# Shared expert of the eight even prompt tiles as four blocks of 256 tokens behind the last routed expert, with the last norm between them

## The chip, the cores and the metric

The kernel runs on one core of a Trainium2 chip. The metric is the device time of one execution in microseconds; the median of three executions is compared.

## The reference, cut to what matters

One layer of a decoder over 2048 prompt tokens and 64 sample tokens of width 1024: a mixer (sliding-window attention and short convolution), a norm, a mixture of experts with one shared expert, a second norm. The change concerns the last two:

```
xt = layer_norm(ALPHA * x + mixer(x))
shared = (silu(xt @ ws_gate) * (xt @ ws_up)) @ ws_down          # 1024 -> 256 -> 1024, every token
routed = sum over the 6 chosen of 64 experts of gate * ((silu(xt @ w_gate[e]) * (xt @ w_up[e])) @ w_down[e])
y = layer_norm(ALPHA * xt + routed + shared)
```

All is float32. A product is made of float32r parts: each operand is split in a high part (rounded, on ScalarE) and a low part (the difference, on VectorE), and high x high, high x low and low x high are summed.

## The kernel before, in words

Tokens lie in 17 tiles of 128 (16 of the prompt, one with the 64 sample tokens). There are four stages, one behind the other, each with its own program per engine and signals between the engines: the mixer, the dense stage, the routed experts, the norm. Every engine works its program in order; the order within a stage is written out by hand.

The dense stage (`stage_dense`) makes step i for tile i. TensorE's order in a step: first half of the output projection of tile i+1 (`project`, 24 products of 512 columns), transposes of the hidden values of tile i-1 (`hidden_T`), transposes of h of tile i (`transpose_h`), second half of the projection, the rank sums of tile i-1 (`rank`), the shared expert's down product of tile i-1 (`down`, 12 products), the router product (`router`), the shared expert's gate and up of tile i (`gate_up`, 24 products of 512 columns), the router's logits (`logits`). VectorE's: split of the hidden values (`hidden`, L1209), split of h (`split_h`, L1198), `ranks` (L1251), `residual` and mean of tile i+1, split of the next cat tile, `accumulate` of tile i-1 (acc = ALPHA * h + shared), `normalise` of tile i+1, `place` (slots of tile i-1 in the routing table), `activate` (sigmoid x gate x up, L1203), `pick` (the choice of experts, L1220 to L1249). ScalarE rounds, scales, and makes sigmoids and square roots. SP loads x and cat of the next tiles and stores acc to `acc_d`; GpSimd stores h to `h_d` and scatters the entries to the table. Steps 1 to 14 are a hardware loop of seven rounds with an odd and an even step; step 0 and the last two tiles are written out.

The expert stage (`stage_experts`) runs 64 experts in pairs, each on up to 256 gathered tokens: rows of `h_d` are gathered by GpSimd, transposed, split; gate and up in two halves f (L1927, L1929: 16 times 512 and 256 columns for 256 tokens), then down (L1905 to L1907) for two token tiles and two column halves, whose sums ScalarE scales (`output`, L1751) and GpSimd adds to `acc_d` by indirect DMA. The chain behind a half is `copy_lo` (L1711, ScalarE), `sums` (L1818), `sigmoid` (ScalarE), `activate`, `hidden` on ScalarE (rounding) and on VectorE (rest). Weights come from memory by SP, 1 MB in each transfer, are rounded by ScalarE (L1733) and split by VectorE (L1842). Behind the loop over pairs (`pairs`) stand the last two experts' ends: L1978 to L1993 for TensorE.

The norm stage (`stage_norm`) starts when all routed sums are in memory and every engine has left the expert stage. SP loads tiles of `acc_d`, ScalarE makes sum and squares of a tile (`statistics`, L2057), VectorE subtracts the mean and multiplies by g (`centre`, L2087), then multiplies by the reciprocal deviation and adds b (`finish`, L2096), SP stores to y. TensorE and GpSimd have no part in it.

## Time and profile before

| | us |
|---|---|
| median of three executions | 2157.96 (2151.61 to 2160.45) |
| profiled execution, own time | 2153.67 |
| its span, first to last instruction | 2151.8 |
| TensorE busy in it | 2041.9 (95%) |
| VectorE, ScalarE, GpSimd busy | 1406.2, 1224.3, 624.8 |

The profile comes from one execution. A timeline row gives the start, the length, the engine (PE TensorE, PEld its weight loads, DVE VectorE, ACT ScalarE, POOL GpSimd, SP the DMA queue of SyncE), the line of the kernel, what is written and read; in brackets how long the engine had been idle and what ended it. Matmuls overlap: their starts tell the pace, not their lengths. The mean granted TensorE clock is 0.978 of full speed.

### The profile page before, as it was taken

What the parts mean: (1) busy time and instruction counts of PE and PEld (TensorE: products, weight loads), DVE (VectorE), ACT (ScalarE), POOL (GpSimd) and SP (SyncE); (2) the same over time, 40 slices, a digit from 0 to 9 for tenths busy, and PEclk for the clock granted to TensorE, in tenths of its full rate; (3) what the DMA queues carried; (4) which work ended last, traced back from release to release, by engine and by line L of the source; (5) the groups of instructions that cost most, each with busy time, mean ns of one, the idle gap of its engine ahead of it and who ended that gap; (6) DMA issues with size and microseconds to landing.
All of it is one profiled execution on the core that took longest, in us unless ns stands there. A gap on an engine that the chain in (4) does not pass through costs nothing. (4 is left out here: it accounts for less than half of the span.)

```text
span 2151.8 us, 36827 instructions
## 1 busy us (share of the span) xinstructions
PE 2041.9 (95%) x11526; PEld 1717.9 (80%) x11526; DVE 1406.2 (65%) x2774; ACT 1224.3 (57%) x2167; POOL 624.8 (29%) x659
## 2 busy tenths in 40 slices
PE   8999999999999999988999999999999999999950
PEld 6777787787778888876888888889988888888840
DVE  6444444444667777777777777777777777776628
ACT  6344344343543333334777777776777777766628
POOL 2111111111013232243444444354333333333210
PEclk9999999999999999999999999999999999999975
DMA  5101101010453232345999999999999999999857
GB/s 223 56 31 37 44 30 37 30 40 32 171 199 118 78 117 78 116 159 176 273 285 306 301 307 292 302 299 293 282 283 294 304 294 284 287 291 280 246 121 300
DMA packets 113978, 413.82 MB, mean 192 GB/s; under 512 B 35872, under 2 KB 40480, under 8 KB 86208
## 3 DMA queue, kind: packets, MB, share of 16 engines
q1 hardware_dynamic: 76032, 290.02, 37.1%
q0 software_dynamic: 37872, 122.90, 24.5%
q8 instruction: 36, 0.59, 0.1%
q14 instruction: 38, 0.31, 0.0%
HBM read 316.91 MB, written 98.12 MB: 193 GB/s over the span
## 5 line engine op out<-in xcount | busy, mean ns | idle before, releaser
L1927 PE MATMUL ex_psU<-ex_xs,ex_guh 128*128 128x384 f32 (+5 forms) x2016 | 621.9, 372 | 0.1
L1929 PE MATMUL ex_psU<-ex_xs,ex_gul 128*128 128x192 f32 (+5 forms) x2016 | 522.6, 259 | 0.0
L1927 PEld LDWEIGHTS ex_psU<-ex_xs,ex_guh 128*128 128x128 f32 x2016 | 378.0, 187 | 49.0 <-issue 17.7
L1929 PEld LDWEIGHTS ex_psU<-ex_xs,ex_gul 128*128 128x128 f32 x2016 | 384.1, 191 | 1.5
L1688 POOL DMA_INDIRECT ex_xg<-h_d,entries x128 | 156.9, 1226 | 486.7 <-issue 238.5
L1671 POOL DMA_INDIRECT acc_d<-ex_y,ex_rows x128 | 215.9, 1687 | 200.8 <-ACT ex_y L1751 172.3
L1751 ACT ACTIVATE ex_y<-ex_psY,ex_use 128x512 f32<-128x512 f32 x254 | 169.8, 682 | 50.9 <-PE ex_psY L1958 26.1
L1818 DVE TENSOR_TENSOR ex_gu<-ex_psU,ex_lo 128x384 f32<-128x384 f32 (+5 forms) x128 | 77.3, 604 | 170.6 <-ACT ex_lo L1711 170.5
L1905 PE MATMUL ex_psY<-ex_dnh,ex_hdh 128*128 128x512 f32 (+3 forms) x412 | 171.7, 417 | 8.5 <-DVE ex_dnl L1842 4.3
L1847 DVE TENSOR_TENSOR ex_xs<-ex_psX,ex_xs 128x512 fp32r<-128x512 f32 (+5 forms) x125 | 130.7, 1046 | 58.8 <-ACT ex_xs L1740 57.8
L720 PE MATMUL mi_psG<-mi_gh,mi_xh 128*128 128x512 f32 x408 | 167.7, 411 | 0.0
L1711 ACT ACTIVATE ex_lo<-ex_psU 128x384 f32<-128x384 f32 (+5 forms) x128 | 66.9, 523 | 173.6 <-PE ex_psU L1929 173.0
L1907 PE MATMUL ex_psY<-ex_dnh,ex_hdl 128*128 128x512 f32 (+3 forms) x412 | 163.7, 397 | 0.0
L1906 PE MATMUL ex_psY<-ex_dnl,ex_hdh 128*128 128x512 f32 (+3 forms) x412 | 162.9, 395 | 0.0
L1842 DVE TENSOR_TENSOR ex_gul<-mi_g_raw,ex_guh 128x1024 fp32r<-128x1024 f32 x128 | 156.0, 1221 | 10.1 <-ACT ex_guh L1733 10.1
L1842 DVE TENSOR_TENSOR ex_gul<-mi_g_place,ex_guh 128x1024 fp32r<-128x1024 f32 x128 | 156.0, 1221 | 7.8 <-ACT ex_guh L1733 7.4
L720 PE MATMUL mi_psG<-mi_gl,mi_xh 128*128 128x512 f32 x408 | 159.7, 392 | 0.0
L720 PE MATMUL mi_psG<-mi_gh,mi_xl 128*128 128x512 f32 x408 | 159.7, 391 | 0.0
L1733 ACT ACTIVATE ex_guh<-mi_g_raw 128x1024 fp32r<-128x1024 f32 x128 | 134.0, 1049 | 11.1 <-PEq L900 11.1
L1733 ACT ACTIVATE ex_guh<-mi_g_place 128x1024 fp32r<-128x1024 f32 x128 | 134.0, 1049 | 0.0
L1913 PE MATMUL ex_psX<-ex_ident,ex_xg 128*128 128x128 f32 x1008 | 130.9, 273 | 2.0 <-DMA ex_xg<-h_d,entries 1.8
L1740 ACT ACTIVATE ex_xs<-ex_psX 128x512 fp32r<-128x512 f32 (+5 forms) x125 | 110.3, 883 | 31.4 <-PE ex_psX L1913 30.2
(411 smaller groups left out, 4241.3 us busy)
## 6 DMA issues: line engine op xcount, KB each, us to landing
mi_g_raw<-w_experts SPq DMA_DIRECT2D x96, 1024.0 KB, 8.0
mi_g_place<-w_experts SPq DMA_DIRECT2D x96, 1024.0 KB, 7.9
mi_xr<-xT SPq DMA_DIRECT2D x17, 512.0 KB, 3.6
acc_d<-de_acc SPq DMA_DIRECT2D x17, 512.0 KB, 3.0
h_d<-de_h POOLq DMA_DIRECT2D x17, 512.0 KB
de_cr<-cat SPq DMA_DIRECT2D x16, 512.0 KB, 6.0
de_xr<-x_rows SPq DMA_DIRECT2D x16, 512.0 KB, 5.3
mi_g_raw<-w_conv SPq DMA_DIRECT2D x6, 1024.0 KB, 16.0
```

The source lines that it names most:

```text
L720: last = nc.tensor.matmul(psG[:, (k + j) % 2, :], a[:, k, kc, :], b[:, j, kc, :], start=(kc == 0 and n == 0), stop=(kc == KC - 1 and n == 2))
L1671: nc.gpsimd.indirect_dma_start(out=io["acc_d"], out_offset=bass.IndirectOffsetOnAxis(ap=rows[0:r, 2 * b + t:2 * b + t + 1].bitcast(U32), a ...
L1688: nc.gpsimd.indirect_dma_start(out=xg[0:r, k, :], out_offset=None, in_=io["h_d"], in_offset=bass.IndirectOffsetOnAxis(ap=ent[0:r, k, 0:1]. ...
L1733: A(hi, src, ACT.Copy).then_inc(s_round if q < 4 else s_dround, 1)
L1751: A(y[0:r, k, half * 512:(half + 1) * 512], sums(u)[at], ACT.Copy, scale=use[at, k, 1:2].bitcast(F32)).then_inc(s_y, 1)
L1842: V.tensor_tensor(lo, src, hi.bitcast(F32), ALU.subtract).then_inc(done, 1)
L1905: nc.tensor.matmul(out, lh, rh, start=start, stop=False)
L1906: nc.tensor.matmul(out, lh, rl, start=False, stop=False)
L1907: return nc.tensor.matmul(out, ll, rh, start=False, stop=stop)
L1913: last = nc.tensor.transpose(rows_T(p, t)[:, kc * P:(kc + 1) * P], xg[:, 2 * b + t, kc * P:(kc + 1) * P], ident[:])
L1927: nc.tensor.matmul(psU[:, f, half, 0:2 * n].rearrange("p (s n) -> p s n", s=2), guh[:, b, kc, c0:c0 + P], rows_split(e)[:, kc, :, 0:n], st ...
L1929: last = nc.tensor.matmul(psU[:, f, half, 0:n], gul[:, b, kc, c0:c0 + P], rows_split(e)[:, kc, 0, 0:n], start=False, stop=(kc == KC - 1))
```

## The change

In the dense stage the even prompt tiles (0, 2, ... 14, `DEFERRED`) no longer run gate and up, hidden and down of the shared expert. `keep_h` on ScalarE writes ALPHA * h for them to acc, and SP stores their split h (high and low, 1 MB for each tile) to a new memory tensor `hT_d`. Odd tiles and the sample tile keep the shared expert; m counts them.

Behind the last routed expert the shared weights are loaded, rounded and split like a 65th expert's, and four blocks of two deferred tiles run (`gate_up_block`, `down_block`). TensorE's order is now gate_up of the last expert, down of the last two, and then (n, f being block and half) G00 G01 G10 D0 G11 G20 D1 G21 G30 G31 D2 D3. The norm stage is gone as a stage; its work stands between the chains of the blocks:

- ScalarE: chains 00, 01, 10; `statistics` 1, 3, 5; `deviations` 0; chain 11; `squares` 0, 2; deviations 1; chain 20; statistics 7, 9; squares 4, 6; deviations 2; chain 21; statistics 11; chain 30; statistics 13; chain 31; statistics 15, 16; deviations 3; squares 8, 10; deviations 4; squares 12, 14; deviations 5.
- VectorE: chains 00, 01, 10; `add` 0, 2; `reciprocals` 0; `scale` 1, 3, 5; chain 11; reciprocals 1; scale 0, 2; chain 20; add 4, 6; `centre` 4, 6; reciprocals 2; scale 7, 9; chain 21; `finish` 4, 6; chain 30; centre 13; chain 31; add 8, 10; centre 15, 16; reciprocals 3; scale 11; finish 13; add 12; finish 16, 15; centre 8, 10; reciprocals 4; finish 8; add 14; finish 10; centre 12, 14; reciprocals 5; finish 12, 14.
- GpSimd multiplies by g and adds b for the eight tiles that VectorE scaled (`ON_POOL`).

```diff
+BLOCKS = PT_TILES // 4
+DEFERRED = range(0, PT_TILES, 2)
+STATS = (1, 3, 5, 0, 2, 7, 9, 4, 6, 11, 13, 15, 16, 8, 10, 12, 14)
+BATCHES = (3, 5, 9, 13, 15, 17)
+ON_POOL = (1, 3, 5, 0, 2, 7, 9, 11)
+ON_DVE = (4, 6, 13, 16, 15, 8, 10, 12, 14)
+STORES = (1, 3, 5, 0, 2, 4, 6, 7, 9, 11, 13, 16, 15, 8, 10, 12, 14)
+LOADS = ((0, 2), (1, 3), (5, 7), (4, 6), (9, 11, 8, 10), (13, 15, 12, 14, 16))
...
+            def store_hT(i, n):
+                sp.wait_ge(S["hT_lo"], i + 1)
+                sp.dma_start(io["hT_d"][bass.ds(n, 1)].rearrange("o p n -> (o p) n"),
+                             hT[:].rearrange("p k s t -> p (k s t)").bitcast(F32)).then_inc(S["hT_stored"], 16)
...
+            def step(i, k, first, m):
                 if not first:
                     load_x(i + 1)
                 load_cat(i + 2)
+                if k == 0:
+                    store_hT(i, 0 if first else m + 1)
                 if not first:
                     store_acc(i - 1, acc)
...
+            def step(i, k, first, m):
                 if first:
                     scale_attention(1)
+                elif k == 0:
+                    hidden(m, psR[:, 128:384])
+                if k == 0:
+                    round_h(i, psT[:], "gu", 0 if first else m + 1)
                 else:
...
+            def keep_h(i):
+                act.wait_ge(S["acc_stored"], 16 * i)
+                A(acc[:], h[:, 0, :], ACT.Copy, scale=ALPHA).then_inc(S["acc"], 1)
...
+                if k == 1:
+                    keep_h(i - 1)
                 copy_router(i)
                 deviation(i + 1)
                 score(i)
-                sigmoid(i, psU[:, 0:FF])
+                if k == 1:
+                    sigmoid(m, psU[:, 0:FF])
...
                 project(i + 1, 1 - k, 0)
                 if first:
                     project(1, 1, 1)
                     pe.wait_ge(S["zero"], 2)
+                elif k == 0:
+                    hidden_T(i - 1, m, psR[:, 128:384])
                 else:
-                    hidden_T(i - 1, psR[:, 128:384])
                     after(pe, S["acc"], i - 1)
                 transpose_h(i, k, psT)
                 if not first:
                     project(i + 1, 1 - k, 1)
-                    pe.wait_ge(S["hid_lo"], i)
+                    if k == 0:
+                        pe.wait_ge(S["hid_lo"], m + 1)
                     rank(i - 1)
                     pe.wait_ge(S["hT_lo"], i + 1)
-                    down(i - 1, psT)
+                    if k == 0:
+                        down(m, psT)
                 else:
                     pe.wait_ge(S["w_lo"], n_w - 1)
                 router(i)
-                gate_up(psU[:], range(KC)).then_inc(S["gu"], 1)
+                if k == 1:
+                    after(pe, S["hid"], m)
+                    gate_up(psU[:], range(KC)).then_inc(S["gu"], 1)
                 logits(i)
                 if first:
                     pe.wait_ge(S["w_lo"], n_w)
...
+            for kind in range(2):
+                hold(sp, s_split, 4 * e - 6 + 2 * kind, s_sp_passed)
+                load_shared(kind)
             load_down(e - 1, 1)
+            hold(sp, s_dsplit, 2 * e - 2, s_sp_passed)
+            load_shared(2)
+            hold(sp, s_split, 4 * e - 2, s_sp_passed)
+            sp.dma_start(ln_g[:], io["ln2_g"].partition_broadcast(P)).then_inc(s_const, 16)
+            sp.dma_start(ln_b[:], io["ln2_b"].partition_broadcast(P)).then_inc(s_const, 16)
+            hold(sp, s_xT, 2 * e, s_sp_passed)
+            load_block(0)
+            hold(sp, s_gu, 2 * e, s_sp_passed)
+            load_block(1)
             hold(sp, s_add, 32 * e, s_sp_passed)
+            load_tiles(0)
+            load_tiles(1)
+            hold(sp, s_gu, 2 * e + 2, s_sp_passed)
+            load_block(2)
+            for n in range(2, 5):
+                load_tiles(n)
+            hold(sp, s_gu, 2 * e + 4, s_sp_passed)
+            load_block(3)
+            hold(sp, s_split, 4 * e + 2, s_sp_passed)
+            load_tiles(5)
+            for i in STORES:
...
+                sp.dma_start(io["y"][i * P:i * P + rows_at(i)], t_of(i)).then_inc(s_stored, 16)
+            sp.wait_ge(s_stored, 16 * TILES)
...
+            pool.wait_ge(s_const, 48)
+            for n, i in enumerate(ON_POOL):
+                pool.wait_ge(s_scaled, n + 1)
+                nc.gpsimd.tensor_tensor(t_of(i), t_of(i), ln_g[:], ALU.mult)
+                pool.drain()
+                nc.gpsimd.tensor_tensor(t_of(i), t_of(i), ln_b[:], ALU.add).then_inc(s_pout, 1)
...
+            def statistics(i):
+                r = rows_at(i)
+                act.drain()
+                act.wait_ge(*tiles_loaded(count, i))
+                A(scratch[0:r], t_of(i), ACT.Copy, accum_out=of(total, i))
+                act.drain()
+                A(of(minus, i), of(total, i), ACT.Copy, scale=-1.0 / D)
+                act.drain()
+                squares(i)
+            def squares(i):
+                if i in DEFERRED:
+                    act.drain()
+                    act.wait_ge(s_added, DEFERRED.index(i) + 1)
+                A(scratch[0:rows_at(i)], t_of(i), ACT.Square, bias=of(minus, i), accum_out=of(square, i)).then_inc(s_square, 1)
+            def deviations(n):
+                at = slice(BATCHES[n - 1] if n else 0, BATCHES[n])
+                act.drain()
+                A(std[:, at], square[:, at], ACT.Sqrt, bias=eps, scale=1.0 / D).then_inc(s_std, 1)
...
+            def add(n, c):
+                i = DEFERRED[2 * n + c]
+                dve.wait_ge(s_dn, 4 * (e + n) + 2 * c + 2)
+                dve.wait_ge(*tiles_loaded(count, i))
+                V.scalar_tensor_tensor(t_of(i), psX[:] if c else psY[:].rearrange("p h n -> p (h n)"), 1.0, t_of(i),
+                                       ALU.mult, ALU.add, accum_out=of(total, i))
+                dve.drain()
+                V.tensor_scalar(of(minus, i), of(total, i), -1.0 / D, None, ALU.mult).then_inc(s_added, 1)
+            def centre(i):
+                dve.wait_ge(s_square, STATS.index(i) + 1)
+                V.scalar_tensor_tensor(t_of(i), t_of(i), of(minus, i), ln_g[0:rows_at(i)], ALU.add, ALU.mult)
+            def reciprocals(n):
+                at = slice(BATCHES[n - 1] if n else 0, BATCHES[n])
+                dve.wait_ge(s_std, n + 1)
+                V.reciprocal(rstd[:, at], std[:, at])
+                dve.drain()
+            def scale(i):
+                V.tensor_scalar(t_of(i), t_of(i), of(minus, i), of(rstd, i), ALU.add, ALU.mult).then_inc(s_scaled, 1)
+            def finish(i):
+                V.scalar_tensor_tensor(t_of(i), t_of(i), of(rstd, i), ln_b[0:rows_at(i)], ALU.mult, ALU.add).then_inc(s_out, 1)
...
+            def gate_up_block(n, f):
+                x = x_block(n)
+                if f == 0:
+                    pe.wait_ge(s_block[n % 2], 16 * e + 32 * (n // 2) + 32)
+                pe.wait_ge(s_sum, 2 * (e + n) + f - 1)
+                for half in range(2):
+                    c0 = half * FF + f * P
+                    for kc in range(KC):
+                        if n == 0 and f == 0 and half == 0 and kc % 2 == 0:
+                            pe.wait_ge(s_split, 4 * e + kc // 2 + 1)
+                        nc.tensor.matmul(psU[:, f, half, :].rearrange("p (s c t) -> p s c t", s=2, c=2), guh[:, 0, kc, c0:c0 + P],
+                                         x[:, :, kc].rearrange("p c s t -> p s c t"), start=(kc == 0), stop=False)
+                        last = nc.tensor.matmul(psU[:, f, half, 0:BLK].rearrange("p (c t) -> p c t", c=2), gul[:, 0, kc, c0:c0 + P],
+                                                x[:, :, kc, 0, :], start=False, stop=(kc == KC - 1))
+                last.then_inc(s_gu, 1)
+            def down_block(n):
+                pe.wait_ge(s_hl, 2 * (e + n) + 2)
+                if n == 0:
+                    pe.wait_ge(s_dsplit, 2 * e + 2)
+                    pe.wait_ge(s_y, 4 * e)
+                for c in range(2):
+                    if n:
+                        pe.wait_ge(s_added, 2 * n - 1 + c)
+                    for half in range(2):
+                        out = psX[:, half * 512:(half + 1) * 512] if c else psY[:, half, :]
+                        for f in range(FC):
+                            last = three(out, hdh[:, n % 2, f, c * P:(c + 1) * P], hdl[:, n % 2, f, c * P:(c + 1) * P],
+                                         dnh[:, 0, f, half * 512:(half + 1) * 512], dnl[:, 0, f, half * 512:(half + 1) * 512],
+                                         f == 0, f == FC - 1)
+                        last.then_inc(s_dn, 1)
+            gate_up(e - 1, 1, 1, BLK)
             for t in range(2):
                 down(e - 2, 0, t, BLK)
-            gate_up(e - 1, 1, 1, BLK)
...
+            for t in range(2):
+                down(e - 1, 1, t, BLK)
+            gate_up_block(0, 0)
+            gate_up_block(0, 1)
+            gate_up_block(1, 0)
+            down_block(0)
+            gate_up_block(1, 1)
+            gate_up_block(2, 0)
+            down_block(1)
+            gate_up_block(2, 1)
+            gate_up_block(3, 0)
+            gate_up_block(3, 1)
+            down_block(2)
+            down_block(3)
```

## Rows read from the trace of the kernel before

**Rows 1.** Windows: length, busy PE, PEld, DVE, ACT, POOL, granted clock, DMA share, GB/s
```profile
2054.40:2064.40 10.00, 5.86 (x14) 4.61 (x15) 1.97 (x4) 2.35 (x5) 0.00 (x0) 0.66 0.39 89
...
2085.00:2098.00 13.00, 0.00 (x0) 0.00 (x0) 0.00 (x2) 0.58 (x2) 3.04 (x2) 0.63 0.72 169
...
2098.00:2151.80 53.80, 0.00 (x0) 0.00 (x0) 46.91 (x58) 43.69 (x94) 0.00 (x0) 0.50 0.78 300
```

**Rows 2.** TensorE's timeline, one dense step (start, length, engine, line, out<-in, shape, count)
```profile
899.85 0.20 PE L1425 MATMUL de_psR<-de_mkb,de_trib 128*128 128x64 bf16 x1
...
899.92 0.48 PE L1398 MATMUL de_psT<-de_dnh,de_hdh 128*128 128x512 f32 x1
...
902.80 1.11 PE L1450 MATMUL de_psR<-de_hT,de_rw 128*128 128x256 f32 x8
...
903.75 0.39 PE L1398 MATMUL de_psU<-de_guh,de_hT 128*128 128x512 f32 x1
...
909.21 0.55 PE L1457 MATMUL de_psR<-de_eye,de_lt 128*128 128x64 f32 x4
...
915.15 0.38 PE L1433 MATMUL de_psR<-de_ident,de_hid 128*128 128x128 f32 x2
...
915.37 1.04 PE L1419 MATMUL de_psT<-de_ident,de_h 128*128 128x128 f32 x8
...
916.16 0.48 PE L1398 MATMUL de_psC<-mi_gh,mi_xh 128*128 128x512 f32 x1
...
921.73 0.20 PE L1425 MATMUL de_psR<-de_mkb,de_trib 128*128 128x64 bf16 x1
```

**Rows 3.** VectorE's timeline in that step; in brackets what it waited for
```profile
900.19 0.23 DVE L1254 TENSOR_TENSOR de_dd<-de_psR,de_base 128x64 f32<-128x64 f32 x1 [3.35 <-PE de_psR L1426]
...
911.33 0.42 DVE L1205 TENSOR_TENSOR de_hid<-de_psU,de_sg 128x256 f32<-128x256 f32 x1
...
912.16 0.22 DVE L1222 TENSOR_TENSOR de_sel<-de_sc,de_rbias 128x64 f32<-128x64 f32 x1
...
916.55 0.42 DVE L1211 TENSOR_TENSOR de_hdl<-de_psR,de_hdh 128x256 fp32r<-128x256 f32 x1
```

**Rows 4.** ScalarE's timeline in that step
```profile
903.95 0.38 ACT L1105 ACTIVATE de_lt<-de_psR 128x256 f32<-128x256 f32 x1 [6.42 <-PE de_psR L1450]
...
907.12 1.28 ACT L1110 ACT_TABLE_LOAD   x1
```

**Rows 5.** TensorE's timeline at the dense stage's two ends
```profile
625.02 0.50 PE L1398 MATMUL de_psA<-mi_gh,mi_xh 128*128 128x512 f32 x1 [0.33 <-DVE mi_xl L1164]
...
939.09 0.47 PE L1398 MATMUL de_psC<-mi_gh,mi_xh 128*128 128x512 f32 x1
...
947.44 1.11 PE L1450 MATMUL de_psR<-de_hT,de_rw 128*128 128x256 f32 x8
```

**Rows 6.** TensorE's timeline behind the routed loop
```profile
2058.54 0.79 PE L1905 MATMUL ex_psY<-ex_dnh,ex_hdh 128*128 128x512 f32 x1 [4.15 <-issue]
...
2064.55 0.39 PE L1907 MATMUL ex_psY<-ex_dnh,ex_hdl 128*128 128x512 f32 x1
```

**Rows 7.** Timelines of ScalarE and VectorE, first half of the last routed expert
```profile
2054.43 0.60 ACT L1711 ACTIVATE ex_lo<-ex_psU 128x512 f32<-128x512 f32 x1 [3.92 <-PE ex_psU L1929]
...
2055.15 0.69 DVE L1818 TENSOR_TENSOR ex_gu<-ex_psU,ex_lo 128x512 f32<-128x512 f32 x1 [3.15 <-ACT ex_lo L1711]
```

**Rows 8.** Timelines of ScalarE and VectorE in the norm
```profile
2129.98 1.04 ACT L2060 ACTIVATE ln_scratch<-ln_t 128x1024 f32<-128x1024 f32 x1
...
2132.76 0.29 ACT L2066 ACTIVATE ln_std<-ln_square,ln_eps 128x1 f32<-128x1 f32 x1
...
2147.17 1.28 DVE L2097 SCALAR_TENSOR_TENSOR ln_t<-ln_t,ln_rstd,ex_ln_b 64x1024 f32<-64x1024 f32 x1
```

**Rows 9.** GpSimd's group of its widest operation; VectorE's timeline, one cast
```profile
L348 POOL TENSOR_TENSOR mi_pr<-mi_pr,mi_rd 128x1024 f32<-128x1024 f32 x16 | 30.3, 1893 | 135.0 <-DVE mi_rd L582 135.0
...
612.61 0.22 DVE L1302 CAST de_trib<-de_trif 128x128 bf16<-128x128 f32 x1
```

435 lines of the change are left out of this document (236 added, 199 removed).

## The prediction

> **What bounds the kernel now.** Start with the windows of the last stretch [rows 1]: from 2085 on TensorE runs nothing. For 13 us the last routed sums are added to memory and a stage boundary is crossed, then the norm takes 53.8 us with VectorE busy 46.91 and ScalarE 43.69. Then read TensorE's timeline over one step of the dense stage [rows 2]: rank, down, router, gate and up, logits, output projection and transposes follow each other without a hole, 21.88 us from rank to rank (899.85 to 921.73). VectorE in the same step waits 3.35 us [rows 3]. So the dense stage is bound by TensorE, the tail by VectorE and ScalarE, and the change moves work from the one to the other. What it is worth is the dense time saved minus the growth of the tail.
>
> **Dense stage: what a step loses.** An even tile no longer runs gate and up, 903.75 to 909.21 = 5.46 us, nor, in the odd step behind it or the even step behind that, its transposes of hidden (915.15 to 915.37 = 0.22) and its down product (899.92 to 902.80 = 2.88 with the rank's tail) [rows 2]. Eight tiles at some 8.5 us would be 68 us; what is late next takes part of it back.
>
> Odd step, whose tile keeps gate and up but has no down and no hidden transpose of the tile before. The down product used to hide the round trip from rank to router: VectorE reads the ranks 0.34 us behind the rank and needs 0.22 [rows 3], so the router can start 0.66 behind it. From there, [rows 2]: router 0.95, gate and up 5.46, logits and first half of the projection 5.94 (909.21 to 915.15), the hidden transpose of this odd tile 0.22, transposes 0.79, second half 5.57. Sum 19.59 from rank to rank.
>
> Even step: down of the odd tile 2.95, router 0.95, then the logits at once, which need ScalarE's copy: 903.95 + 0.38 stands 1.53 behind the router's start [rows 4], with some 0.1 for the signal 1.63, so 0.68 is waited. Then 5.94 + 0.79 + 5.57. Sum 16.88.
>
> Is VectorE still ahead? From a rank to the end of pick it takes 16.70 us now (899.85 to 916.55), 0.83 of it activate (911.33 to 912.16) [rows 3]. Even step: 15.87, then split_h 1.2 (1024 columns, as in [rows 8]), done at 17.1, while TensorE's next rank starts at 16.88 and VectorE is wanted at 17.22. It is covered by 0.1 us only. The odd step has 1.8 us to spare. If nothing covers, each tenth late costs a tenth in six steps. ScalarE's new keep_h (a copy of 1024 columns, 1.04 as its like in [rows 8]) lies in its 6 us wait for the router. The new store of 1 MB sits in SP's queue ahead of the store of acc and the loads of the next x and cat; it starts before the rank and those are issued some 7 us behind it, so it is through. GpSimd's six scatters per step are behind the table as before.
>
> Ranks of steps 1 to 14 are 13 periods apart: now 13 x 21.88 = 284.4, then 7 x 19.59 + 6 x 16.88 = 238.4. That is **46.0 us**. Step 0 gives nothing for its 5.46: the next projection waits for VectorE's split of cat at 625.02 anyway [rows 5]; the missing hidden transpose of step 1 gives 0.2. Behind step 14 the second half of the last projection starts 17.36 us behind the rank (921.73 to 939.09); then it waits for the mask of tile 14, at 15.3: 2.1 us. Behind it down(14) goes from in front of the router (947.44) [rows 5] and ScalarE's deviation comes about 1 us sooner. Dense stage together **49.3 us**; from both sides 43 (VectorE a full microsecond late in each even step) to 53 (the waits of 0.66 and 0.68 not seen).
>
> **Tail, step by step**, on the clock of the profile before, without the dense gain.
> - TensorE stops 4.15 us at the end of the routed loop [rows 6] and then runs at half clock (granted 0.66 on average in the window from 2054.4 [rows 1]) until some 5.9 us behind the restart; 512 columns take 0.23 us at full clock (5.46 / 24 [rows 2]) and twice that or a little less at half. The hole stays, since the loop stays. gate_up of the last expert, now first, takes 8.3 at that clock, the four down units of each of the two last experts 11.0 and 0.7 of waits for ScalarE's copies: the blocks start at 2078.5. The second hole (to 2077) is gone.
> - A block's gate and up is twice 16 x 768 columns = 2 x 5.5, its down 24 x 512 = 5.5 (columns as in [rows 2]). Alone, TensorE would be done at 2078.5 + 66 = 2144.8.
> - A chain of one block half is copy 0.60, sums 0.69 [rows 7], then sigmoid, two products, rounding, split of 256 columns at 0.42 each [rows 3]: about 3.6 us over two engines. The statistics of a tile cost ScalarE 2.78 (2129.98 to 2132.76), the squares alone 1.3 [rows 8], each change between sigmoid and square root a table of 1.28 [rows 4]. VectorE: add 1.3 and 0.15, centre and finish 1.2 each [rows 8]. scale, with one tensor input, was not seen at this size; the cast of 128 columns in 0.22 costs what 64 would at the rate of the 256-column rows, so I take 0.69, not 1.2 [rows 3, 9].
> - ScalarE is through chain (1,0) at 2098.4. Three statistics 8.4, table and root 1.6: 2108.4. VectorE waits for that root, scales three tiles, and only then does chain (1,1): down of block 1 starts at 2113.9 instead of 2111.7.
> - Roots for tiles 0 and 2 at 2117.6, chain (2,0) done 2122.3, adds to 2125.3; ScalarE's two statistics and two squares to 2130.0, root 2131.6; centre twice, scale twice, sums (2,1) at 2134.0. TensorE's gate_up (3,1) waits for it, 3.5 us, and loses 2.3 at half clock: 2141.9.
> - Chain (2,1), finish twice, chain (3,0), centre(13) behind its statistics (2146.0), chain (3,1) to 2149.1, adds to 2152.1. Down of block 3 starts at 2150.6 and ends at 2158.4.
> - From there VectorE's queue has one hole of 0.9 us: 13 centres and finishes, two adds, a scale and three reciprocals, 21.3 us: 2173.4. The last store lands 3.4 behind, as now (finish from 2147.17 to 2148.45, span 2151.8 [rows 1, 8]): **2177.0**, a tail 25.2 us longer.
> - GpSimd's two operations per tile (1.89 each [rows 9]), sixteen in all, run beside VectorE. No row has a two-input VectorE operation under such a one. Bounds: 0, or they exclude each other; then most chain links from (1,1) to (3,0) wait 1.2 to 1.9 and the walk ends at 2185.4, 8.4 later. Nothing in the rows leans to either end, so I take the middle, 4.2.
>
> The Trainium skill, "SBUF — State Buffer", section "Who interferes with whom", says that a VectorE instruction with two SBUF inputs and a GpSimd instruction that reads SBUF block each other for the whole instruction. No run here shows it yet. By it the sum takes the upper end, 8.4, instead of 4.2.
>
> **Sum.** 2151.8 - 49.3 + 25.2 + 4.2 = 2131.9 of span. The profiled execution took 2153.67 around its span of 2151.8, so 2133.8. It lies 4.3 below the median of the three runs (2157.96); on the median's scale 2138.
>
> **Rivals.**
> - Full exclusion of VectorE and GpSimd in the tail: 4.2 more, **2142**. For it: VectorE and GpSimd both read SBUF tiles all through the tail. Against: nothing in the rows.
> - The dense stage turns to VectorE: 0.1 us of cover in the even steps. At 43 us saved, **2144**. For it: the thin cover and the drains of the loop's end; against: VectorE's step repeats to a hundredth.
> - The tail stays close to TensorE: waits for tables and statistics overlap better than in my walk, tail 15 longer instead of 29: **2124**. Against: both queues are in order, and ScalarE and VectorE are already at 44 and 47 of 54 us with the norm alone [rows 1].
> - Slower than before: transfers set the tail. From 2063 to the end 8.4 MB of blocks, 8.7 MB of tiles and 8.7 MB of stores go through the 16 engines. The norm moved 300 GB/s on average, the stretch of scattered adds just before 169 [rows 1]. Below 186 GB/s the bytes alone end the tail behind 2201, where the dense gain is used up; at 169 they end at 2215, which gives **2172**. Against: only the first loads meet scattered adds, and the norm's rate holds with loads and stores together.
>
> **Numbers.** Forecast 0.50, full exclusion 0.20, dense turned to VectorE 0.12, short tail 0.08, transfers 0.10. Bounds together: dense 53 and tail 16 gives 2121, dense 43 and tail 38.6 (upper end of GpSimd, scale at 1.2) gives 2154. Range 2118 to 2156. A measurement of this kernel can tell about 0.5%, 10.8 us, from no change. Faster than 2147.2: nearly all of the first and of the short tail, most of the two between: 0.79. Within: 0.12. Slower: 0.09, the transfers.
>
> **What would show it.** In the dense stage, rank to rank alternating 19.6 and 16.9 instead of 21.88, the router waiting for VectorE in odd steps and the logits for ScalarE in even ones; VectorE's wait before the ranks close to nothing in even steps. In the tail, TensorE starting blocks some 24 us behind the loop's end and idle three times (before down 1, gate_up (3,1), down 3) by 2 to 5 us with its clock halved behind the longer ones; VectorE the engine without holes at the end; GpSimd's operations near 1.9 us if nothing excludes, longer, or VectorE's two-input ones longer, if it does. Wrong would be: no alternation in the dense stage (the gain fell to VectorE), waits of ScalarE on loads in the tail (transfers), or TensorE ending last with the stores.

## The result, and the profile after

The changed kernel takes **2172.56 us** (median of 12 runs, 2165.5 to 2178.11), the kernel before 2157.66 (12 runs beside them, 2150.01 to 2166.84): ratio 1.0069, 95% interval 1.0052 to 1.0086. It is 0.7% slower, some 15 us. The forecast was 2138, its range 2118 to 2156. In what follows a ratio to the kernel before is turned into microseconds by 2157.7; a difference between two changed kernels goes over two such ratios and is known to some 5 us.

The profiled execution has a span of 2172.4 us where the sum said 2131.9, so 40.5 us are to be found. They can be split at marks that both traces have (the first routed product is the first product of the routed experts):

| us | before | after | change | predicted |
|---|---|---|---|---|
| start of the dense stage | 591.47 | 594.24 | +2.8 | 0 |
| from there to the first rank | 45.74 | 48.06 | +2.3 | -0.2 |
| 13 periods, rank to rank | 284.5 | 252.0 | -32.5 | -46.0 |
| to the last rank | 46.11 | 47.76 | +1.7 | -3.1 |
| to the first routed product | 27.0 | 28.3 | +1.3 | 0 |
| from there to the first block | - | 1080.3 | | 1083.7 |
| first block to the end | - | 121.7 | | 102.7 |

The predicted 1083.7 and 102.7 are the forecast's block start at 2078.5 and tail end at 2181.2, on the clock of before, whose first routed product is at 994.8. The first line isn't the change: the other profiled executions, whose kernels are alike up to there, start the dense stage at 591.1 to 591.8 or at 593.7 to 594.7. The first routed product comes 24.4 us earlier than before; without the 2.8 of the start the dense stage gave 27.2 of the 49.3 us (in one execution). The last line costs 19 us more than foreseen.

TensorE's timeline over an even step and the odd one behind it (columns: start, duration, engine and line, operation, out<-in, count, idle before it and what ended it), to be read against [rows 2, 4]:

```profile
778.18 0.20 PE L1455 MATMUL de_psR<-de_mkb,de_trib 128*128 128x64 bf16 x1
...
781.14 1.11 PE L1479 MATMUL de_psR<-de_hT,de_rw 128*128 128x256 f32 x8
782.72 0.66 PE L1486 MATMUL de_psR<-de_eye,de_lt 128*128 128x64 f32 x4 [0.47 <-ACT de_lt L1122]
784.69 0.50 PE L1428 MATMUL de_psA<-mi_gh,mi_xh 128*128 128x512 f32 x1 [1.31 <-DVE mi_xl L1191]
...
796.62 0.20 PE L1455 MATMUL de_psR<-de_mkb,de_trib 128*128 128x64 bf16 x1
...
797.33 1.19 PE L1479 MATMUL de_psR<-de_hT,de_rw 128*128 128x256 f32 x8 [0.48 <-DVE de_dd L1285]
...
816.35 0.20 PE L1455 MATMUL de_psR<-de_mkb,de_trib 128*128 128x64 bf16 x1
```

The alternation is there: odd 19.73 (predicted 19.59), even 18.44 (predicted 16.88). The logits' wait of 0.47 was in the sum; the 1.31 in front of the projection was not. VectorE's queue in the same even step shows where it comes from:

```profile
778.52 0.23 DVE L1285 TENSOR_TENSOR de_dd<-de_psR,de_base 128x64 f32<-128x64 f32 x1 [2.38 <-PE de_psR L1456]
779.18 1.28 DVE L1198 SCALAR_TENSOR_TENSOR de_t<-de_psC,de_rc,de_t 128x1024 f32<-128x1024 f32 x1 [0.33 <-issue]
780.59 1.23 DVE L1202 SCALAR_TENSOR_TENSOR de_t<-de_xr,de_t 128x1024 f32<-128x1024 f32 x1
...
782.22 1.28 DVE L1207 SCALAR_TENSOR_TENSOR de_centred<-de_t,de_minus,mi_g_raw 128x1024 f32<-128x1024 f32 x1
783.42 1.22 DVE L1191 TENSOR_TENSOR mi_xl<-de_cr,mi_xh 128x1024 fp32r<-128x1024 f32 x1
```

The split of cat (mi_xl) for the tile after next stands behind ranks, residual and centre, and ends 6.5 us behind the rank. TensorE is there after 5.2. Two of the six even steps took 20.05 and 20.08: in them the clock fell behind that wait. The windows of the stretch behind the wait, of such a step and of the one above (columns as in [rows 1]; PEclk is the first figure behind the busy times):

```profile
744.90:751.00 6.10, 6.10 (x20) 4.87 (x21) 5.45 (x30) 2.23 (x4) 1.01 (x2) 0.72 0.67 214
784.60:790.00 5.40, 5.31 (x23) 4.43 (x24) 4.83 (x23) 2.33 (x4) 0.58 (x1) 1.00 0.62 199
```

Step 0 and the end of the stage, TensorE's timeline, against [rows 5]:

```profile
627.72 0.80 PE L1428 MATMUL de_psA<-mi_gh,mi_xh 128*128 128x512 f32 x1 [4.11 <-DVE mi_xl L1191]
...
909.23 0.20 PE L1455 MATMUL de_psR<-de_mkb,de_trib 128*128 128x64 bf16 x1 [1.81 <-DVE de_mkb L1274]
...
923.20 1.66 PE L1449 MATMUL de_psA<-de_ident,de_h 128*128 128x128 f32 x8 [3.33 <-DVE de_h L1219]
...
931.42 2.04 PE L1479 MATMUL de_psR<-de_hT,de_rw 128*128 128x256 f32 x8 [3.40 <-DVE de_dd L1285]
```

Before, the same projection of step 0 waited 0.33 [rows 5]. At the end the forecast's first gain is there: the second half of the last projection starts 15.0 us behind its rank (909.30) where it was 17.36, and 15.3 was said. Then it is lost again. The last two waits have their like in the kernel before, 0.99 and this one:

```profile
960.03 1.19 PE L1450 MATMUL de_psR<-de_hT,de_rw 128*128 128x256 f32 x8 [3.04 <-DVE de_dd L1254]
```

What is new is the clock behind them. Windows from that router to the last rank, before (one) and after (two, columns as above):

```profile
960.03:967.84 7.81, 7.31 (x39) 6.00 (x40) 4.86 (x38) 1.38 (x4) 3.65 (x4) 1.00 0.54 221
```

```profile
931.42:937.10 5.68, 5.68 (x18) 4.81 (x18) 2.10 (x17) 0.38 (x1) 1.96 (x2) 0.50 0.69 280
937.10:942.06 4.96, 4.26 (x22) 3.31 (x21) 2.93 (x20) 0.99 (x3) 3.88 (x4) 0.99 0.03 3
```

In the tail TensorE's three holes are at the three named places (down of block 1, gate_up (3,1), down of block 3), but 8 to 10 us long where 2 to 5 were said:

```profile
2093.31 0.79 PE L2175 MATMUL ex_psY<-ex_dnh,ex_hdh 128*128 128x512 f32 x1 [8.30 <-DVE ex_hdl L2014]
...
2120.99 0.80 PE L2260 MATMUL ex_psU<-ex_x_odd,ex_guh 128*128 128x512 f32 x1 [8.63 <-DVE ex_gu L1997]
...
2143.63 0.76 PE L2175 MATMUL ex_psY<-ex_dnh,ex_hdh 128*128 128x512 f32 x1 [9.50 <-DVE ex_stats L2092]
```

VectorE's queue around the first hole and a little later, then GpSimd's over that later stretch:

```profile
2085.80 0.17 DVE L2101 RECIPROCAL ex_stats<-ex_stats 128x3 f32<-128x3 f32 x1 [11.07 <-ACT ex_stats L1947]
...
2102.72 1.46 DVE L2003 TENSOR_TENSOR ex_gu<-ex_gu,ex_lo 128x256 f32<-128x256 f32 x1 [0.48 <-ACT ex_lo L1830]
2104.25 2.47 DVE L2008 TENSOR_TENSOR ex_gu<-ex_gu 128x256 f32<-128x256 f32 x1
2107.29 1.98 DVE L2014 TENSOR_TENSOR ex_hdl<-ex_gu,ex_hdh 128x256 fp32r<-128x256 f32 x1 [0.56 <-ACT ex_hdh L1837]
2109.19 1.21 DVE L2089 SCALAR_TENSOR_TENSOR ex_t<-ex_psY,ex_t 128x1024 f32<-128x1024 f32 x1
```

```profile
2101.04 2.85 POOL L1813 TENSOR_TENSOR ex_t<-ex_t,ex_ln_g 128x1024 f32<-128x1024 f32 x1
...
2104.04 2.40 POOL L1815 TENSOR_TENSOR ex_t<-ex_t,ex_ln_b 128x1024 f32<-128x1024 f32 x1
2106.40 2.58 POOL L1813 TENSOR_TENSOR ex_t<-ex_t,ex_ln_g 128x1024 f32<-128x1024 f32 x1
2109.12 2.42 POOL L1815 TENSOR_TENSOR ex_t<-ex_t,ex_ln_b 128x1024 f32<-128x1024 f32 x1
```

An operation on 256 columns that takes 0.42 alone takes 1.46 to 2.47 here: each of the three ends 0.28 to 0.29 us behind the end of a GpSimd instruction. The add at 2109.19, which reads one operand from PSUM, runs in its 1.21 right through GpSimd's. And in the first line VectorE stands 11.07 us in front of the first reciprocal, with a finished product of TensorE waiting behind it in the queue.

### The profile page after: what moved, and what is told of

The parts are those of the page before. It is cut to its first block, busy times and chain, and to the rows that moved or that the text cites. A ratio compares the mean times of both kernels' runs of the same rounds, so it can differ in the third digit from the quotient of the medians.

```text
span 2172.4 us, 37064 instructions
## 1 busy us (share of the span) xinstructions
PE 2063.9 (95%) x11574; PEld 1735.0 (80%) x11574; DVE 1420.0 (65%) x2780; ACT 1243.9 (57%) x2169; POOL 679.4 (31%) x675
## 4 chain that ended last, share of the span: by engine, by line
PE 49%; DVE 2%; DMA 2%; ACT 1%; issue 1%; DVEq 1%; SPq 0%; ACTq 0%; POOL 0%; POOLq 0%
PE ex_psU L2197 20%; PE ex_psU L2199 9%; PE ex_psX L2183 5%; PE ex_psY L2177 4%; PE ex_psY L2175 4%; PE ex_psY L2176 4%; PE ex_psY L2228 2%; DMA acc_d<-ex_y,ex_rows 1%; DMA ex_t<-acc_d 1%; ACT ex_scratch L1942 0%; DVE ex_t L2105 0%; DVE ex_t L2108 0%; DVE ex_t L2096 0%; ACT ex_scratch L1932 0%; DVE ex_gu L2008 0%
## 5 line engine op out<-in xcount | busy, mean ns | idle before, releaser
L1795 POOL DMA_INDIRECT ex_xg<-h_d,entries x128 | 161.8, 1264 | 492.2 <-issue 267.0
L1778 POOL DMA_INDIRECT acc_d<-ex_y,ex_rows x128 | 221.2, 1728 | 179.0 <-ACT ex_y L1865 139.9
L2175 PE MATMUL ex_psY<-ex_dnh,ex_hdh 128*128 128x512 f32 (+3 forms) x432 | 179.9, 416 | 18.3 <-DVE ex_stats L2092 9.5
L1865 ACT ACTIVATE ex_y<-ex_psY,ex_use 128x512 f32<-128x512 f32 (+5 forms) x256 | 171.1, 682 | 40.5 <-PE ex_psY L2228 26.1
L1997 DVE TENSOR_TENSOR ex_gu<-ex_psU,ex_lo 128x512 f32<-128x512 f32 (+5 forms) x136 | 82.7, 608 | 170.4 <-ACT ex_lo L1825 170.3
L1825 ACT ACTIVATE ex_lo<-ex_psU 128x512 f32<-128x512 f32 (+5 forms) x136 | 71.6, 527 | 180.5 <-PE ex_psU L2199 172.0
L2177 PE MATMUL ex_psY<-ex_dnh,ex_hdl 128*128 128x512 f32 (+3 forms) x432 | 171.6, 397 | 0.0
L2176 PE MATMUL ex_psY<-ex_dnl,ex_hdh 128*128 128x512 f32 (+3 forms) x432 | 170.8, 395 | 0.0
L2021 DVE TENSOR_TENSOR ex_gul<-mi_g_raw,ex_guh 128x1024 fp32r<-128x1024 f32 x132 | 160.6, 1219 | 13.7 <-ACT ex_guh L1847 13.7
```

What stands on the lines that cost most here:

```text
L1778: nc.gpsimd.indirect_dma_start(out=io["acc_d"], out_offset=bass.IndirectOffsetOnAxis(ap=rows[0:r, 2 * b + t:2 * b + t + 1].bitcast(U32), a ...
L1795: nc.gpsimd.indirect_dma_start(out=xg[0:r, k, :], out_offset=None, in_=io["h_d"], in_offset=bass.IndirectOffsetOnAxis(ap=ent[0:r, k, 0:1]. ...
L1865: A(y[0:r, k, half * 512:(half + 1) * 512], sums(u)[at], ACT.Copy, scale=use[at, k, 1:2].bitcast(F32)).then_inc(s_y, 1)
L2021: V.tensor_tensor(lo, src, hi.bitcast(F32), ALU.subtract).then_inc(done, 1)
L2175: nc.tensor.matmul(out, lh, rh, start=start, stop=False)
L2176: nc.tensor.matmul(out, lh, rl, start=False, stop=False)
```

## Experiments

Twelve kernels, each timed against the kernel before on the same chip. "First block to end" is read from the one profiled execution of a kernel; where the work behind the first block is the changed kernel's (runs 2 and 3) it is 120.8 and 121.3 for 121.7.

**1. The dense half alone** (dense_alone). The expert and norm stages are those of the kernel before; the dense stage is the changed one.

```
-        stage_experts(nc, io, ov, front["raw"], first_entries, s_ent, s_weights, s_sp_passed, s_passed)
+        first = stage_experts(... of the kernel before ...)
+        stage_norm(nc, io, first, s_norm)
```

> The dense stage of the changed kernel (with the store of hT) in front of the expert and norm stages of the kernel before; the shared expert of the eight even tiles is left out. It prices the first half of the change by itself. Theory: in an even step the next projection waits for VectorE's split of cat, which stands behind ranks, residual and centre in its queue; the loop gives back 32.5 us and the first step and the end lose 5 to 8 of it, so 2132 us (24 to 27 under before), and the tail then has cost the changed kernel 39 to 42 us. Rival, my prediction's account: the dense stage gives 49 us and the changed kernel lost all of it behind, 2109 us.

Measured 2118.53 us, ratio 0.9841 (0.9803 to 0.9879): 34 us under the kernel before, 26 to 42 with the interval. More than the 24 to 27 expected, less than the forecast's 49. The expectation rested on one execution, whose 24.4 held 2.8 us of a late start and more of a lowered clock: in this run's profile the dense stage up to the first routed product gives 32.1 us where the changed kernel's gave 27.2, and 2.5 of the difference lie behind the last router, where the clock stayed at 1.00 (8.11 us to the last rank for 10.64). The tail of the changed kernel has then cost (1.0069 - 0.9841) x 2157.7 = 49 us, where the forecast had 29.

**2. The split early in every step** (cat_first).

```
                 else:
+                    split_cat(i + 2, k)
                     ranks(i - 1)
                 residual(i + 1)
-                split_cat(i + 2, k)
```

> The changed kernel with VectorE's split of cat for tile i+2 moved ahead of ranks (into 2.4 us in which VectorE sits idle). Theory (place of the split): TensorE's 1.31 us wait before the projection goes in 7 steps, and with it the two steps in which the clock then fell (1.6 us each): even period 18.44 to 17.1, 9 to 13 us faster than the changed kernel, 2160 to 2163 us. Rival: another wait (the router's copy, the mask, the h of the next tile) takes its place, under 4 us gained, 2169 or more.

Measured 2164.12, ratio 1.0046 (1.003 to 1.0062): 5 us faster than the changed kernel. Even steps fell to 17.02, odd ones rose to some 20.5. The rival had the right kind of thing: in odd steps nothing stands between rank and router, and a split in front of ranks holds the router up. Its wait, [0.48] in the timeline above, in this kernel:

```profile
793.68 1.19 PE L1481 MATMUL de_psR<-de_hT,de_rw 128*128 128x256 f32 x8 [1.20 <-DVE de_dd L1285]
```

**3. The split early in even steps alone** (cat_even).

```
                 else:
+                    if k == 0:
+                        split_cat(i + 2, k)
                     ranks(i - 1)
```

> The changed kernel with the split of cat ahead of ranks in even steps alone. In the run with it in every step the even period fell from 18.44 to 17.02 and the odd one rose from 19.73 to 20.46, since the router there waits for ranks (1.20 us where it was 0.48). Theory: odd steps stay at 19.73, even ones at 17.02, the 13 periods from 252.0 to 240 us, 9 to 12 us faster than the changed kernel, 2161 to 2164 us. Rival: with even steps shorter the odd ones lengthen anyway (the work of VectorE over two steps is the bound), no better than the run with both, 2164 to 2167.

Measured 2158.47, ratio 1.0011 (0.9996 to 1.0027): 12.5 us faster than the changed kernel. An even and an odd step of its timeline, 17.04 and 19.72, and no step at 20:

```profile
770.81 0.20 PE L1458 MATMUL de_psR<-de_mkb,de_trib 128*128 128x64 bf16 x1
...
787.85 0.20 PE L1458 MATMUL de_psR<-de_mkb,de_trib 128*128 128x64 bf16 x1
788.56 1.18 PE L1482 MATMUL de_psR<-de_hT,de_rw 128*128 128x256 f32 x8 [0.48 <-DVE de_dd L1285]
...
807.57 0.20 PE L1458 MATMUL de_psR<-de_mkb,de_trib 128*128 128x64 bf16 x1
```

**4. The dense half alone, with that split** (dense_alone_even): edits 1 and 3 together.

> The dense stage alone (the even tiles' shared expert left out, expert and norm stages of the kernel before), with the split of cat early in even steps. It prices the dense stage that my prediction described. Theory: the missing 15 us of the dense gain were the wait for the split and the clock behind it: 10 to 14 us under the run without that order, 2105 to 2112 us, 44 to 51 under the kernel before (predicted 49). Rival: another 10 us are lost elsewhere in the dense stage, 2113 to 2119 us.

Measured 2110.73, ratio 0.9784 (0.9768 to 0.98): 46.6 us under the kernel before (43 to 50). By the time this is nearly the forecast's 49.3. The profile says less, 38.3 us up to the first routed product (40.8 and 42.8 in runs 3 and 10, with the same dense stage): the 13 periods give 44.2 of the forecast 46.0, and the two ends with the passage behind them, which should have given 3.3, lose 5.9 here. So the loop is as forecast, the ends are not.

**5. Chains first** (chain_first), the order of the two queues in the tail; VectorE's part, ScalarE's is alike.

```
             add(0, 1)
+            chain(1, 1)
             reciprocals(0)
...
-            chain(1, 1)
...
             add(1, 1)
+            chain(2, 1)
             centre(4)
...
-            chain(2, 1)
...
             chain(3, 0)
-            centre(13)
-            chain(3, 1)
             add(2, 0)
             add(2, 1)
+            chain(3, 1)
+            centre(13)
```

> The changed kernel with the order of VectorE's and ScalarE's queues in the tail changed: each activation chain that TensorE waits for stands ahead of the statistics, scales and centres that it stood behind. Theory (queue order): TensorE's three holes of 8.3, 8.6 and 9.5 us close and with them the half clock behind each; 15 to 25 us faster than the changed kernel, 2148 to 2157 us. Rival (work bound): VectorE has 58 us of work in the last 72 us, the norm's instructions only end later, 3 to 8 us gained, 2165 to 2169 us.

Measured 2171.27, ratio 1.0063 (1.004 to 1.0087): no difference from the changed kernel. The theory was wrong in its size. The first hole did close and the second shrank to 3.54, but all of it came back in one place, TensorE's wait in its timeline, while two centres and two finishes in VectorE's took 6.75 and 6.64 where two take 2.5 undisturbed (2.46 to 2.48 at the end of the changed kernel's tail):

```profile
2139.29 0.80 PE L2175 MATMUL ex_psY<-ex_dnh,ex_hdh 128*128 128x512 f32 x1 [23.38 <-DVE ex_hdl L2014]
```

```profile
2109.53 6.75 DVE L2096 SCALAR_TENSOR_TENSOR ex_t<-ex_t,ex_stats,ex_ln_g 128x1024 f32<-128x1024 f32 x2
...
2117.90 6.64 DVE L2108 SCALAR_TENSOR_TENSOR ex_t<-ex_t,ex_stats,ex_ln_b 128x1024 f32<-128x1024 f32 x2
```

From the first block to the end it took 121.6 us, against 121.7.

**6. Without GpSimd's arithmetic** (no_gpsimd).

```
-                nc.gpsimd.tensor_tensor(t_of(i), t_of(i), ln_g[:], ALU.mult)
-                pool.drain()
-                nc.gpsimd.tensor_tensor(t_of(i), t_of(i), ln_b[:], ALU.add).then_inc(s_pout, 1)
```

> The changed kernel without GpSimd's sixteen instructions in the norm (the products with g and sums with b of eight tiles are left out). Theory (exclusion): while GpSimd works on tiles, VectorE's instructions with all operands in SBUF take 1.4 to 2.5 us in place of 0.42, and 2.2 in place of 1.28; summed over the trace of after this is 20 us, most of it in front of TensorE's waits: 12 to 20 us faster than the changed kernel, 2152 to 2161 us. Rival (my price): the exclusion costs 4 us, 2168 us.

Measured 2154.3, ratio 0.9989 (0.9973 to 1.0005): 17 us faster than the changed kernel. Groups by shape on VectorE in the tail (count, busy us, mean ns, idle before), first of the changed kernel, then of this one; in order: finish, centre, scale, second product, split, first product, add from PSUM:

```profile
L2108 DVE SCALAR_TENSOR_TENSOR ex_t<-ex_t,ex_stats,ex_ln_b 128x1024 f32<-128x1024 f32 x8 | 14.3, 1806 | 0.1
L2096 DVE SCALAR_TENSOR_TENSOR ex_t<-ex_t,ex_stats,ex_ln_g 128x1024 f32<-128x1024 f32 x8 | 11.8, 1508 | 4.6 <-ACT ex_scratch L1942 4.6
L2105 DVE TENSOR_SCALAR ex_t<-ex_t,ex_stats 128x1024 f32<-128x1024 f32 x8 | 10.9, 1402 | 0.3
L2008 DVE TENSOR_TENSOR ex_gu<-ex_gu 128x256 f32<-128x256 f32 x8 | 7.5, 934 | 0.6
L2014 DVE TENSOR_TENSOR ex_hdl<-ex_gu,ex_hdh 128x256 fp32r<-128x256 f32 x8 | 6.6, 825 | 4.1 <-ACT ex_hdh L1837 4.1
...
L2003 DVE TENSOR_TENSOR ex_gu<-ex_gu,ex_lo 128x256 f32<-128x256 f32 x8 | 5.4, 678 | 3.9 <-ACT ex_lo L1830 3.9
...
L2089 DVE SCALAR_TENSOR_TENSOR ex_t<-ex_psY,ex_t 128x1024 f32<-128x1024 f32 x4 | 4.9, 1215 | 0.0
```

```profile
L2102 DVE SCALAR_TENSOR_TENSOR ex_t<-ex_t,ex_stats,ex_ln_b 128x1024 f32<-128x1024 f32 x8 | 10.1, 1279 | 0.1
L2090 DVE SCALAR_TENSOR_TENSOR ex_t<-ex_t,ex_stats,ex_ln_g 128x1024 f32<-128x1024 f32 x8 | 10.1, 1278 | 6.2 <-ACT ex_scratch L1936 6.2
L2099 DVE TENSOR_SCALAR ex_t<-ex_t,ex_stats 128x1024 f32<-128x1024 f32 x8 | 6.1, 811 | 0.3
...
L2083 DVE SCALAR_TENSOR_TENSOR ex_t<-ex_psY,ex_t 128x1024 f32<-128x1024 f32 x4 | 4.9, 1218 | 0.0
L2002 DVE TENSOR_TENSOR ex_gu<-ex_gu 128x256 f32<-128x256 f32 x8 | 3.4, 426 | 0.6
```

The three products and splits of 256 columns are each 3.4 us for eight without GpSimd. The differences are 4.2 + 1.7 + 4.8 + 4.1 + 3.2 + 2.0 = 20.0 us, with the 64-row finish (2.0 for 1.3) 20.7, and 17 of it reached the end. First block to end: 104.3 us, 17.4 under the changed kernel's.

**7. GpSimd writes and reads nothing** (gpsimd_writes).

```
-                nc.gpsimd.tensor_tensor(t_of(i), t_of(i), ln_g[:], ALU.mult)
-                pool.drain()
-                nc.gpsimd.tensor_tensor(t_of(i), t_of(i), ln_b[:], ALU.add).then_inc(s_pout, 1)
+                for _ in range(2):
+                    nc.gpsimd.memset(t_of(i), 0.0)
+                    pool.drain()
+                nc.gpsimd.memset(t_of(i)[:, 0:512], 0.0).then_inc(s_pout, 1)
```

> The changed kernel with GpSimd's two instructions per tile (product with g, sum with b) replaced by three that write constants into the tile and read nothing; the eight tiles are left unnormed. Order, waits and semaphores of GpSimd stay. Theory (the shared resource is the reading of SBUF): VectorE's instructions with two SBUF inputs take 0.42 and 1.28 us again, and the time is that of the run without GpSimd, 17 us under the changed kernel, 2152 to 2158 us. Rival (any GpSimd activity, or the semaphores, holds VectorE): stretched instructions as before wherever a constant is written, 2163 or more.

Measured 2156.01, ratio 1.0 (0.9983 to 1.0017): 15 us faster than the changed kernel, within 2.4 us of no GpSimd at all. First block to end: 106.0 us. The same groups on VectorE, scale, finish and second product:

```profile
L2109 DVE SCALAR_TENSOR_TENSOR ex_t<-ex_t,ex_stats,ex_ln_b 128x1024 f32<-128x1024 f32 x8 | 10.1, 1279 | 0.1
L2106 DVE TENSOR_SCALAR ex_t<-ex_t,ex_stats 128x1024 f32<-128x1024 f32 x8 | 8.5, 1107 | 0.3
...
L2009 DVE TENSOR_TENSOR ex_gu<-ex_gu 128x256 f32<-128x256 f32 x8 | 3.4, 426 | 0.6
```

GpSimd was at work for 21.3 us (42 in the changed kernel), and the instructions with two SBUF inputs are at their undisturbed durations, also where they run beside GpSimd's (a product at 2101.59 and a split at 2102.58 take 0.42 and 0.43 inside constants written from 2101.50 to 2103.53). Only the scale, with one input, is still stretched (1107 for 811).

**8. The norm all on VectorE** (on_vector), the rest of the order kept.

```
-            reciprocals(0)
-            scale(1)
-            scale(3)
-            scale(5)
+            centre(1)
+            centre(3)
+            centre(5)
+            reciprocals(0)
+            finish(1)
+            finish(3)
+            finish(5)
```

> The changed kernel with the norm of the eight tiles that went through GpSimd done by VectorE like the other nine (centre and finish, 1.28 us each, in place of a scale of 0.77 and GpSimd's two instructions); GpSimd does nothing in the tail. Theory (exclusion costs more than GpSimd brings): without GpSimd the tail was 17 us shorter, VectorE's 14 us more work falls in part into its idle time: 2160 to 2166 us. Rival (GpSimd relieves VectorE): VectorE has no room, 14 us on top of 2154 and the holes longer: 2170 us or more.

Measured 2161.13, ratio 1.0026 (1.0009 to 1.0044): 9 us faster than the changed kernel, although VectorE has 14 us more to do by undisturbed durations. First block to end: 108.9 us.

**9. The same with another order of both queues** (vector_ordered): the beginning of VectorE's, against edit 8.

```
+            centre(3)
             add(0, 0)
             add(0, 1)
             centre(1)
-            centre(3)
-            centre(5)
-            reciprocals(0)
-            finish(1)
...
             chain(1, 1)
...
             chain(2, 0)
             add(1, 0)
+            centre(0)
             add(1, 1)
...
+            centre(2)
+            reciprocals(0)
+            finish(3)
```

The first root is of tiles 3 and 1 alone here, and no longer waits for the third tile.

> The norm of all tiles on VectorE, and the queues of VectorE and ScalarE in the tail put in another order (each chain that TensorE waits for ahead of the norm's instructions not yet ready, adds and centres brought forward, the square roots in six batches as before or fewer). Theory (order matters once nothing excludes): 6 to 12 us faster than the same work in the old order, 2150 to 2158 us. Rival (work bound): order gained 1 to 3 us with GpSimd in it and does no more here, 2158 to 2165.

Measured 2153.27, ratio 0.9983 (0.9967 to 1.0): 9 us under the same work in the old order. First block to end: 101.5 us.

**10. All three** (combined): the split early in even steps, and edit 9.

> The split of cat early in even steps, the norm all on VectorE, and the new order together. Theory (the losses add): 9 to 12 us under the run with the ordered tail alone, 2139 to 2148 us, which is under the kernel before (2157.7) by 0.4 to 0.9%. Rival (a shorter dense stage is given back): 2150 or more.

Measured 2139.16, ratio 0.9937 (0.9914 to 0.996): 14 us under the kernel before and 28 under the changed one. First block to end: 100.4 us. TensorE's idle times from 2080 on are all that is left of the three holes:

```profile
2095.47 0.50 PE L2177 MATMUL ex_psY<-ex_dnh,ex_hdh 128*128 128x512 f32 x1 [3.04 <-DVE ex_hdl L2008]
2099.24 0.50 PE L2177 MATMUL ex_psX<-ex_dnh,ex_hdh 128*128 128x512 f32 x1 [0.75 <-DVE ex_stats L2086]
```

**11. Step 0 filled** (combined_busy).

```
+                if first:
+                    gate_up(psU[:], range(KC))
                 if k == 1:
```

> The combined version with gate and up kept in step 0 (its result unused), where TensorE otherwise waits 4.1 us for the split of cat and comes back at half clock. Theory (clock): the wait is filled and the projection behind it starts at the same time but at full clock; from the start of the dense stage to the first rank 45.7 us as in the kernel before in place of 47.5 to 48; 2 us faster than combined, under what the timing can tell, so the profile decides. Rival: the half clock comes from something else than the wait, 47.5 or more, no difference.

Measured 2139.79, ratio 0.9925 (0.9908 to 0.9942), no difference that can be measured. In the profile the projection's wait (3.51 us in combined) is gone and the stretch from the stage's start to the first rank is 46.3 us, against 47.6 in combined and 45.7 before. 1.3 of the 1.8 us came back, in one execution each; the granted clock from 624 to 630 is 1.00 here and 0.54 in combined, so the half clock came with the wait. In the twelve other profiled executions of changed kernels, which all wait there (3.39 to 4.43 us), the stretch is 47.0 to 48.3.

**12. Fewer loads in the tail** (fewer_loads).

```
-            load_block(2)
...
-            load_block(3)
```

> The changed kernel without the loads of hT of blocks 2 and 3 (they compute with blocks 0 and 1's rows), 4.2 MB less in the tail where the transfers run at over 400 GB/s from 2067 to 2092. Theory (queue order): the loads matter only through the root of the first three tiles, whose third load lands at 2081.4 and which VectorE's queue waits for; it lands 2 to 4 us sooner, TensorE's first hole is as much shorter, and part of it survives to the end: 0 to 4 us faster, 2168 to 2172 us. Rival (transfers set the tail): 10 us faster or more, 2162 us.

Measured 2170.47, ratio 1.0061 (1.0044 to 1.0077): 2 us, within the interval. In its profile ScalarE waits 0.60 us for loads, where it waited 1.69 for the first and 2.96 for the third tile, and VectorE's wait for the first root is 4 us shorter than the 11.07 of the changed kernel:

```profile
2088.24 0.18 DVE L2099 RECIPROCAL ex_stats<-ex_stats 128x3 f32<-128x3 f32 x1 [7.10 <-ACT ex_stats L1945]
```

TensorE's first hole fell from 8.30 to 4.83, and first block to end took 117.7 us for 121.7: in the profile the 4 us arrive. (The whole execution was long all the same, since its first block starts 1086.8 us behind the first routed product, not 1080.3, in code that is the same up to there.) The timing can't tell 2 from 4.

## Why the prediction was wrong

**The even step.** The step that failed is "Even step: [...] so 0.68 is waited. Then 5.94 + 0.79 + 5.57. Sum 16.88." It put the projection straight behind the logits. What the projection needs of VectorE, the split of cat, had been named for step 0 [rows 5] and was not asked about in the loop: without gate and up TensorE is at the projection 5.2 us behind the rank, where it was 9.7, and VectorE's queue up to the split is 6.5 us long. "Is VectorE still ahead?" was asked of the whole round (15.87 plus 1.2 against 16.88), where it was right, and not of each thing that TensorE waits for inside it. By the trace this is 6 x 1.56 us, of which moving the split gives back 1.41 each; two of the even steps lost 1.6 more at a lower clock; seven odd steps were 0.14 longer: 13.6 of the 40.5 us. Runs 3 and 4 show it: with the split moved even steps are 17.02 to 17.04, none at 20, and the 13 periods give 44.2 us where 46.0 was forecast.

**Both ends of the dense stage.** The term that is missing is TensorE's clock behind a wait, which the walk of the tail had ("loses 2.3 at half clock") and the dense stage had not. The 3.1 us to be gained behind step 14 became 1.7 lost. The places came out in the main: 2.4 gained where 2.1 was said, h of the next tile 0.45 sooner where 1 was said, and the last router, which waited 3.04 before and 3.40 now, 0.4 later. But the products behind the two long waits (3.33 and 3.40) ran at granted clocks of 0.63 and then 0.50, where before they ran at 1.00 behind 0.99 and 3.04: 4.59 us for 3.32 and 10.64 for 7.81, 4.1 of the 4.8 us. What releases the drop stays open: behind the same 3.40 four of the other profiled executions ran the last stretch at 1.00 (7.85 to 8.11 us) and six at 0.72 to 0.74 (10.31 to 10.65). The passage to the routed experts has the same: twelve down products took 4.44 us at 0.62 for 2.91 at 1.00. Step 0 was right in its place (the projection starts 7.37 us behind the router in both kernels) and had no term for the clock behind a wait of 4.11 in place of 0.33: 627.7 to 633.3 ran at a granted clock of 0.50, and from the projection to the first rank it took 14.58 for 12.19. With the two long even steps the lowered clock is 11 of the 22 us that the dense stage and the passage fell short of the forecast, in this execution.

**GpSimd beside VectorE.** The step that failed is "Bounds: 0, or they exclude each other; [...] 8.4 later. Nothing in the rows leans to either end, so I take the middle, 4.2." The rival of full exclusion had the mechanism, and even its 8.4 was half of the 17 us that run 6 measured. Two sizes were off. GpSimd's instructions take 2.5 and 2.7 us on average here, not 1.89. And the price was put on the links of the chains alone, once each, while scales, centres and finishes pay too (1402, 1508 and 1806 ns on average for 811, 1278 and 1279), and three instructions of one link in a row each wait for another GpSimd instruction (1.46, 2.47, 1.98).

The Trainium skill, "SBUF — State Buffer", section "Who interferes with whom", says that a VectorE instruction with two SBUF inputs contends with a GpSimd instruction that reads SBUF, over ports that are an exclusive lock, that one SBUF input doesn't contend outside the 2-port modes, and that GpSimd's writes alone leave a two-input instruction alone. Runs 6 and 7 agree in all three: 426 ns for 934, 1215 and 1218 ns for the add from PSUM with and without GpSimd, 426 under GpSimd's writes.

**Order of the queues.** The three holes were foreseen at their places but by the walk's durations. The first has for the most part another cause than GpSimd: VectorE stood 11.07 us in front of reciprocals(0). The walk had a wait there too, but the root came 5.2 us later behind the start of the blocks than walked (35.1 for 29.9), 4.65 of it because ScalarE waited 1.69 and 2.96 us for the loads of the first and the third tile, which the walk had in time. With fewer loads the profile is 4.0 us shorter from the first block on (run 12). Run 5's order brought nothing: while VectorE's work was stretched, the holes it closed opened again as one. With nothing stretched, another order gave 9 us (runs 8 and 9), part of it perhaps because the first root no longer waits for the third tile. The orders of run 5 and run 9 aren't the same, so that the same order is worth more without GpSimd is argued, not shown.

**What held.** The odd step (19.73 for 19.59); the stop at the end of the routed loop (3.42 for 4.15) and the start of the blocks, 23.5 us behind its beginning where some 24 was said; VectorE all but without a hole at the end; scale nearer to 0.69 than to 1.2 (0.81). The transfers (the rival of 2172, whose time came out by chance) did not set the tail: they moved 415 GB/s from 2067 to 2092, where the rival needed less than 186, and 4.2 MB less brought 2 us by the time and 4 in the profile, not the rival's 10. Without GpSimd, and with an order that suits, the tail costs (0.9937 - 0.9784) x 2157.7 = 33 us more than before, give or take 6; the walk had 25. From the first block to the end its profile has 100.4 us, where the walk had 98.5 (102.7 without the 4.2 for GpSimd).

**The sum.** Of the 40.5 us the trace gives 13.6 to the dense loop, 2.5 to step 0, 4.8 to the stage's end, 1.3 to the passage behind it and 2.8 to a start that wasn't the change's; the stretch from the first block on took 19.0 more, the one before it 3.4 less. That is 40.6, the last tenth by rounding. The 19.0 are 13.2 for GpSimd (17.4 by run 6's profile, 4.2 in the forecast) and 5.8 besides, near the 4.0 of the late loads. Why the routed loop took 3.4 less stays open; over eleven profiled executions that stretch, from the first routed product to the first block, took 1078.7 to 1086.8 us.

## What to carry to other kernels

When work is taken off an engine that was the bound, list every semaphore it waits for in the shortened stretch and ask of each where its producer stands in its own queue; that the producer's whole round is short enough says nothing of it. Before giving GpSimd arithmetic on tiles beside a busy VectorE, count VectorE's instructions with two SBUF inputs in that stretch: each can cost a whole GpSimd instruction, and here 14 us more work for VectorE was cheaper. A hole in the bound engine is worth closing only if the engine that made it has room (run 5). A wait that is new or longer on TensorE needs a second term, for the clock behind it: in the dense stage of the profiled execution it was some 11 us, more than the 9.4 of the six even steps that waited for the split.
